# Gate tiles as a stage of their own in seven-product form, attention in one row of 32 steps with the Fourier output product between its pieces

## What is computed

```
hx    = modulate(rms_norm(x, norm1_g), sh1, sc1)
fx, qx, kx, vx = split_projection(hx @ w_in)            # 4 x 512 columns
qx, kx = axial_rope(rms_norm(qx)), axial_rope(rms_norm(kx))
y_four = real(fft2(fx))                                 # 4 groups of 128 channels, over 1024 tokens
y_attn = neighbourhood_attention(qx, kx, vx, kc, vc, rpb)   # 8 heads of 64, window 8 rows x 16 columns, and 256 context keys
gates  = sigmoid(hx @ w_gate)                           # 1024 x 1024 by 1024 x 2048, halves g_f and g_a
merged = g_f * (y_four @ w_fo) + g_a * (y_attn @ w_ao)
x      = x + g1 * (merged @ w_o)
x      = x + g2 * sqrelu_mlp(modulate(rms_norm(x, norm2_g), sh2, sc2))
```

## Time and profile before

| | |
|---|---|
| median of 3 runs | 2571.37 us (2571.21 to 2572.49) |
| span of the profiled execution | 2569.7 us, which is 1.7 us under the median (no time of its own is given for it) |
| PE busy | 2551.7 us, 99% of the span |
| DVE busy | 1753.3 us, 68% |
| ACT busy | 1186.7 us, 46% |
| POOL busy | 208.6 us, 8% |
| DMA | 406.66 MB, mean 158 GB/s |

### The profile page before, as it was taken

The page is one execution under the profiler, slowest core; times in us unless marked ns, Lnnn a source line. Parts: engine busy times, 40 slices in busy tenths (PEclk is TensorE's granted clock), DMA queues, the critical chain, the costliest instruction groups (busy, mean ns, idle before and its releaser), DMA issues.

```text
span 2569.7 us, 41859 instructions
## 1 busy us (share of the span) xinstructions
PE 2551.7 (99%) x16868; PEld 2146.6 (84%) x16868; DVE 1753.3 (68%) x2491; ACT 1186.7 (46%) x1870; POOL 208.6 (8%) x248
## 2 busy tenths in 40 slices
PE   8999999999999999999999999999999999999999
PEld 7888888887888888888989778977887888888887
DVE  7555554569999979798625664666667777778563
ACT  6454445545444443457332443344545555554331
POOL 2232222300000001022000000000000000000000
PEclk9999999999999999999999999999999999999999
DMA  4212211236777799962433221121642444497763
GB/s 160 75 51 77 66 42 35 91 111 199 239 256 250 276 372 321 342 245 85 150 106 99 72 74 51 54 74 54 237 153 93 157 148 156 148 349 257 250 221 135
DMA packets 290913, 406.66 MB, mean 158 GB/s; under 512 B 15776, under 2 KB 162720, under 8 KB 290720
## 3 DMA queue, kind: packets, MB, share of 16 engines
q1 hardware_dynamic: 276464, 352.07, 40.2%
q0 software_dynamic: 14256, 51.91, 6.0%
HBM read 314.79 MB, written 89.13 MB: 157 GB/s over the span
## 4 chain that ended last, share of the span: by engine, by line
PE 79%; DVE 2%; ACT 1%; issue 0%; DMA 0%; DVEq 0%; ACTq 0%; SPq 0%
PE ps L1006 22%; PE ps L939 7%; PE ps L937 7%; PE ps L941 7%; PE ps L609 3%; PE ps L593 3%; PE ps L596 3%; PE ps L1193 3%; PE ps L719 2%; PE ps L723 2%; PE ps L721 2%; PE ps L1194 2%; PE ps L1198 2%; PE ps L1168 1%; PE ps L1021 1%; PE ps L1147 1%
## 5 line engine op out<-in xcount | busy, mean ns | idle before, releaser
L937 PE MATMUL ps<-Bh,Ah 128*128 128x512 f32 x896 | 349.6, 390 | 1.4 <-ACT vb L1764 1.4
L939 PE MATMUL ps<-Bh,Al 128*128 128x512 f32 x896 | 348.8, 389 | 1.5 <-DVE Al L2400 1.5
L2163 DVE TENSOR_TENSOR Wlo<-Wraw,Whi 128x1024 fp32r<-128x1024 f32 x100 | 122.4, 1240 | 206.8 <-ACT Whi L1566 206.3
L941 PE MATMUL ps<-Bl,Ah 128*128 128x512 f32 x640 | 249.0, 389 | 0.0
L1786 ACT ACTIVATE ftr_h<-ftr_r 128x1024 fp32r<-128x1024 f32 x112 | 118.8, 1060 | 241.5 <-DMA ftr_r<-b_scratch 241.5
L719 PE MATMUL ps<-Whi,Hh 128*128 128x256 f32 x736 | 212.2, 288 | 0.0
L1006 PE MATMUL ps<-ftr_h,wgt_h 128*128 128x512 f32 x848 | 210.1, 390 | 0.0
L1006 PE MATMUL ps<-ftr_l,wgt_h 128*128 128x512 f32 x848 | 209.4, 389 | 0.0
L1006 PE MATMUL ps<-ftr_h,wgt_l 128*128 128x512 f32 x848 | 209.4, 389 | 0.0
L723 PE MATMUL ps<-Whi,Hl 128*128 128x256 f32 x736 | 208.2, 283 | 0.0
L721 PE MATMUL ps<-Wlo,Hh 128*128 128x256 f32 x736 | 208.2, 283 | 0.0
(11 more groups left out here) (390 smaller groups left out, 5471.7 us busy)
## 6 DMA issues: line engine op xcount, KB each, us to landing
b_scratch<-qb SPq DMA_DIRECT2D x224, 256.0 KB, 3.0
wgt_r<-in_m_w SPq DMA_DIRECT2D x112, 512.0 KB, 4.5
ftr_r<-b_scratch SPq DMA_DIRECT2D x112, 512.0 KB, 6.0
pair<-in_m_w SPq DMA_DIRECT2D x128, 256.0 KB, 3.3
Wraw<-in_w_in SPq DMA_DIRECT2D x56, 512.0 KB, 4.1
mraw<-in_w_ada POOLq DMA_DIRECT2D x48, 512.0 KB, 4.4
mraw<-in_m_w1T POOLq DMA_DIRECT2D x32, 512.0 KB, 6.4
other<-in_m_w SPq DMA_DIRECT2D x32, 512.0 KB, 5.3
```

What stands on the lines that cost most here:

```text
L937: e.matmul(o, h[:, k, :], Bh[x][:, k, :], start=first and k == 0, stop=False, skip_group_check=not first)
L939: e.matmul(o, l[:, k, :], Bh[x][:, k, :], start=False, stop=False, skip_group_check=not first)
L941: i = e.matmul(o, h[:, k, :], Bl[x][:, k, :], start=False, stop=k == 3, skip_group_check=not first)
L2163: e.tensor_tensor(Wlo[n % 4][:], Wraw[n % 2][:], Whi[n % 4][:].bitcast(F), ALU.subtract).then_inc(*S("w_lo", "v").tick(n))
```

## The change

- The gates leave the attention steps. They become a stage of 56 products of 12 matmuls (`SEQG`, eight columns of seven) between the channel part and the projections, with 672 matmuls of 512 columns in place of 768. The sums of activation blocks that it needs (`Th`/`Tl` 5, 6, 7, 4) are made by POOL, DVE and ACT before and during it: 10 DVE operations of 128x2048, 4 ACT copies of 128x2048, on POOL 4 of 128x512 and 2 of 128x2048. Weight blocks come in quarters of 256 KB, with the same sums on DVE as in the MLPs, and three of four outputs are added on DVE from copies that ACT makes.
- The result of the channel part is no longer split at once: ACT copies it to `Yr`, one transfer of 2048 KB writes it to `y_scratch`, since its place is needed, and one of 2048 KB reads it back (`Yb`) when the projections are done. Then ACT makes `Yh` and DVE `Yl`.
- The projections of both halves come first, then all 32 attention steps in one row. `pv` comes a step later (two buffers `pt`). Between the two `tr` of a step stands a piece of 6 matmuls of the Fourier output product (`fo_piece`), a half tile in two steps.
- ACT copies 768 columns of the first head's transposed probabilities instead of 256, DVE only those of the second head.
- Weights of `w_ao` are fed at steps 8, 16 and 24 by all three engines.

```diff
+        SEQG = [(x, 0) for x in (1, 5, 6, 2, 7)]
+        for q in range(1, 8):
+            SEQG += [(1, q), (5, q), (4, q - 1), (6, q), (3, q - 1), (2, q), (7, q)]
+        SEQG += [(4, 7), (3, 7)]
+        NG = len(SEQG)
+        GSTEP = {x: s for s, x in enumerate(SEQG)}
+        GOUT = {2: (0, 0, 0), 7: (1, 1, 1), 4: (2, 1, 0), 3: (3, 0, 1)}
...
+            def gate_product(s):
+
+                x, q = SEQG[s]
+                if x == 1:
...
+                elif x in (6, 7, 4):
+                    pe.wait_ge(S("gate_copy").at(GSTEP[{6: 1, 7: 6, 4: 7}[x], q]))
+                elif x == 3:
+                    pe.wait_ge(S("gc_sum").at(4 * q + 1))
...
+                pe.wait_ge(S("a_part_hi").at((1, s)), S("a_part_lo").at((1, s)))
+                if x > 3:
+                    pe.wait_ge(S("t_hi").at((5, 6, 7, 4).index(x)), S("t_lo").at((5, 6, 7, 4).index(x)))
+                for k, (bh, bl) in enumerate(of):
+                    e.matmul(o, h[:, k, :], bh, start=first and k == 0, stop=False, skip_group_check=not first)
+                    e.matmul(o, l[:, k, :], bh, start=False, stop=False, skip_group_check=not first)
+                    i = e.matmul(o, h[:, k, :], bl, start=False, stop=k == 3, skip_group_check=not first)
+                i.then_inc(*S("ps_full", b).tick(key))
...
+            def fo_piece(p):
+
+                i, late = divmod(p, 2)
+                m, hf = divmod(i, 2)
+                if i % 4 == 0 and not late:
+                    fo_w[0] = weight(("w_fo", m), 4)
+                n, wh, wl = fo_w[0]
+                t, c, ms = psum[3][:, 512:1024], HALF[hf], slice(128 * (m % 2), 128 * (m % 2) + 128)
+                if not late:
+                    if i:
+                        pe.wait_ge(S("fo_free").at(i - 1))
+                    else:
+                        empty(3, filled[3])
+                    pe.wait_ge(S("w_hi").at(n), lo_of(n))
+                for k in ((2, 3) if late else (0, 1)):
+                    pe.wait_ge(S("fy_hi").at(k), S("fy_lo").at(k))
+                    e.matmul(t, wh[:, k, ms], Yh[:, k, c], start=k == 0, stop=False)
+                    e.matmul(t, wl[:, k, ms], Yh[:, k, c], start=False, stop=False)
+                    x = e.matmul(t, wh[:, k, ms], Yl[:, k, c], start=False, stop=k == 3)
+                if late:
+                    x.then_inc(*S("fo_full").tick(i))
+                    GL[n] = i
...
-                pe.wait_ge(S("kcT").at(0), S("vc").at(0))
-                for i in range(NP):
-                    qk(half, i)
-                    for g in gate_steps(half, i) or [None]:
-                        steps_ = iter(()) if g is None else gate(half, g)
-                        next(steps_, None)
-                        if i:
-                            tr(half, i - 1, 0)
-                        next(steps_, None)
-                        if i:
-                            tr(half, i - 1, 1)
-                        next(steps_, None)
-                        if i:
-                            pv(half, i - 1)
+            for i in range(NP):
+                qk(i)
+                if i:
+                    tr(i - 1, 0)
+                    fo_piece(i - 1)
+                    tr(i - 1, 1)
+                if i > 1:
+                    pv(i - 2)
+            fo_piece(NP - 1)
...
+            sp.wait_ge(*(out_at(("chan", par, j)) for par, j in CHAN))
+            e.dma_start(y_d, Yr[:]).then_inc(*S("y_out").tick(0, 16))
+            for s in range(NG):
+                gate_step(*SEQG[s])
+                if s >= 3:
+                    gate_out(s - 3)
...
+            sp.wait_ge(full_at(((1, "v"), 1)), S("y_out").at(0))
+            e.dma_start(Yb[:], y_d).then_inc(*S("y_in").tick(0, 16))
+            for i in range(1, NP + 1):
+                pair = (i - 1) // 8 + 1
+                if i % 8 == 4 and pair < 4:
+                    sp.wait_ge(S("soft_max").at((i - 1, 1)))
+                    load_bias(pair, be, "be", biasE)
+                if i % 8 == 0 and pair < 4:
+                    sp.wait_ge(S("soft_max").at((i - 1, 1)))
+                    load_bias(pair, bm, "bm", biasM)
+                if i % 2 == 0:
+                    fo_out(i // 2 - 1)
+                    if i % 8 == 0:
+                        feed(upto(("w_fo", i // 4 - 2)))
...
+            def gate_copy(s):
+
+                x, q = SEQG[s]
+                if x not in (1, 6, 7, 4):
+                    return
+                act.wait_ge(gproduct_full(s), S("y_out").at(0))
+                if x == 4:
+                    if q >= 2:
+                        act.wait_ge(S("moved", 2 + 4 * (q % 2)).at((2, q - 1)))
+                    e.activation(gst[q % 2][2][:], psum[q % 2][:, HALF[0]], ACT.Copy).then_inc(*S("gate_copy").tick(s))
+                    return
+                back = 2 if x == 6 else 1
+                if q >= back:
+                    act.wait_ge(S("gc_sum").at(4 * (q - back) + {1: 0, 6: 3, 7: 1}[x]))
+                e.activation({1: p1b, 6: gwb[q % 2], 7: gvb}[x][:], psum[q % 2][:, HALF[0]], ACT.Copy).then_inc(
+                    *S("gate_copy").tick(s))
+
+            ga_part(0)
+            chan_out(1, 0)
+            ga_part(1)
+            ga_part(2)
+            chan_out(0, 1)
+            t_hi(7)
+            chan_out(1, 1)
+            for n in range(NG + 1):
+                if n:
+                    gate_copy(n - 1)
+                if n + 3 < NG:
+                    ga_part(n + 3)
+                if n == 4:
+                    t_hi(4)
...
+            table(LOG)
+            for i in range(NP):
+                if i > 2:
+                    o_out(i - 3)
+                if i:
+                    turned(i - 1, 0)
+                soft(i, 0)
+                if i:
+                    turned(i - 1, 1)
+                soft(i, 1)
+                if i == 0:
+                    for k in range(4):
+                        fy_hi(k)
+                elif i % 2 == 0:
+                    fo_copy(i // 2 - 1)
+                if i and i % 8 == 0:
+                    feed(upto(("w_fo", i // 4 - 2)))
...
+            t_lo(5)
+            dve.wait_ge(full_at(("ctx_k1", "T")), H2.lo_at(7))
+            t_part(0, Tr[6][:], block(Hh, 4, 1), Tr[5][:], ALU.subtract)
+            e.tensor_tensor(Tr[6][:], Tr[6][:], block(Hl, 4, 1), ALU.add).then_inc(*S("t_raw").tick((1, 1)))
...
+            ga_sum(1)
+            ga_part(0)
+            dve.wait_ge(S("t_pool").at((1, 0)))
+            t_part(1, Tr[7][:], block(Hh, 4, 1), block(Hh, 0, 1), ALU.subtract)
+            e.tensor_tensor(Tr[7][:], Tr[7][:], Tlow[:], ALU.add).then_inc(*S("t_raw").tick((2, 1)))
+            ga_part(1)
+            ga_sum(2)
+            ga_part(2)
+            t_lo(7)
...
+            for i in range(NP):
+                if i:
+                    norm(i - 1, 1)
+                soft(i, 0)
+                soft(i, 1)
+                if i:
+                    turned(i - 1)
+                norm(i, 0)
+                if i == 0:
+                    for k in range(4):
+                        fy_lo(k)
+                elif i % 8 == 0:
+                    feed(upto(("w_fo", i // 4 - 2)))
...
+            for k in range(4):
+                pool.wait_ge(S("normed").at((5, 0, k)), S("normed").at((5, 1, k)))
+                i = e.tensor_tensor(Tr[5][:, k, :], HT[:, k, HALF[1]], HT[:, k, HALF[0]], ALU.subtract)
+                i.then_inc(*S("t_pool").tick((0, k)))
+            pool.wait_ge(S("xs").at(7), S("t_hi").at(0), S("t_lo").at(0), S("t_raw").at((1, 0)))
             for b in range(2):
                 e.memset(g4(Z[0][1][b])[:, :, 0].bitcast(F), 0.0).then_inc(*S("z_zero").tick(b))
+            block = lambda t, rows, tokens: t[:, rows:rows + 4, HALF[tokens]].bitcast(F)
+            pool.wait_ge(full_at(("dft", 1, 1)), H2.lo_at(7))
+            e.tensor_tensor(Tlow[:], block(Hl, 4, 1), block(Hl, 0, 1), ALU.subtract).then_inc(*S("t_pool").tick((1, 0)))
+            pool.wait_ge(full_at(("chan", 0, 1)))
+            e.tensor_tensor(Tr[4][:], block(Hh, 4, 0), block(Hl, 4, 0), ALU.add).then_inc(*S("t_pool").tick((2, 0)))
...```

How the order changes at three places. First ACT, from the last DFT outputs to the start of what follows the channel part. Before (`Yh` is the channel result, `fo` the output tiles):

```order
L1991 ACTIVATE Z_247<-ps 128x1024
L1977 ACTIVATE Yh<-ps 128x4x256 [waits s_ps_full_0]
L1999 ACTIVATE Z_241<-mid_259 128x4 [waits s_mid_hi]
L1977 ACTIVATE Yh<-ps 128x4x256 [waits s_ps_full_1]
L1977 ACTIVATE Yh<-ps 128x4 [waits s_ps_full_2]
L1977 ACTIVATE Yh<-ps 128x4x255
L1977 ACTIVATE Yh<-ps 128x4x256 [waits s_ps_full_3]
L1566 ACTIVATE Whi_55<-Wraw_53 128x1024 [waits s_ps_full_1,s_w_raw_0]
L2010 ACTIVATE fo_261<-ps 128x1024 [waits s_ps_full_0]
L2010 ACTIVATE fo_262<-ps 128x1024
L1566 ACTIVATE Whi_56<-Wraw_54 128x1024 [waits s_ps_full_3,s_w_raw_1]
```

(36 more changed lines are left out.)

602 lines of the change are left out of this document (331 added, 271 removed).

## The result

The changed kernel takes 2599.8 us (median; 2598.7 to 2602.2) against 2571.9 us: 1.011 times as long, 95% interval 1.0096 to 1.0125. The profiled execution spans 2598.7 us where that of before spans 2569.7, 29.0 us more. The forecast was 2593.9 (2560 to 2617), slower with 0.81.

The account below looks back on a forecast made before the run. The prediction took PE, busy 99% of the span, as the bound. Its terms, -32.0 + 5.3 + 9.4 + 14.3 + 19.2 + 0 + 6.3 = +22.5 us, moved the median from 2571.4 to 2593.9 us, range 2560 to 2617.

Parts of the forecast that it names:

- PE's own work: Whole kernel: 96 matmuls fewer (21.8 us) and less loss where kinds of matmul alternate, together 32.0 us off PE.
- term of 10.2 us for alternation: Attention steps: loss where kinds of matmul alternate falls from 0.47 to 0.15 us, 32 x 0.32 = 10.2 us less.
- Ahead of the channel part: Before Hl and the DFT: POOL sums slow DVE, and added sums delay the DFT's third weight; +5.3 us, bounds 0 and 8.
- The third gate product: Gate stage: PE waits for the p1b copy, which stands behind the write to y_out; +9.4 us, bounds 4.5 and 14.
- The start of the row: First attention steps: the read of Yb, its splits, norm and soft leave PE idle 14.3 us, bounds 10.6 and 19.6.
- the read half hidden, the splits not: Start of the attention row: the lower bound of that wait, 10.6 us.
- Three weights in the row: Steps 8, 16, 24: issue, landing and splits of a weight idle PE 3 x 6.4 = 19.2 us, bounds 0 and 24.
- The rest of the row: Other attention steps: PE bounds them against DVE and ACT, at zero waits.
- hand-overs bound the row: Rival, attention steps: DVE and PE so close that half a microsecond a step is lost; +14 us, 2608, chance 0.13.
- Half rate: Matmuls after the two longest waits (gate product, row start) run at half rate: 2 x 3.15 = 6.3 us, bounds 0 and 15.8.
- the slow rate comes back after every wait: Rival: half rate also follows the three weight waits in the row, adding 3 x 3.15 us; 2603, chance 0.13.
- The landings are hidden: Rival: 29.6 us of transfer landings (write, read of Yb, three weights) are hidden; sum -13.4 us, 2558, chance 0.13.

Follow-up runs that it names:

- sixth experiment: Changed kernel with the sums for Tr5 and Tr4 made by VectorE instead of GpSimd: 2596.1 us, 1.0093 times the kernel before.
- fifth experiment: Changed kernel without the four Yl operations of VectorE, PE multiplying Yh twice instead: 2596.1 us, 1.0091 times the kernel before.
- first experiment: Changed kernel with the three attention-row weights split five steps later (13, 21, 29), loads issued where they were: 2583.6 us, 1.0046 times the kernel before.

## Why the prediction was right, and where its sizes were off

The direction and the places were right; the sum was 6.5 us short on the span (22.5 against 29.0). By its parts:

1. *PE's own work*, -32.0: measured about -25.7. The 96 matmuls fewer hold, and so do gate products 2.72 us apart (the fourth starts at 1327.82, the fifth at 1330.55). The step that failed is the term of 10.2 us for alternation, "I take 0.15 for the one remaining alternation". Without any gain there an edge step would be 10.02 - 24 x 0.227 + 1.36 = 5.93 us and a middle step 6.61; they take 5.80 and 6.50. So 0.12 us a step came back in these two (0.10 over eight steps on end) and not 0.32: 3.3 to 3.9 us in all. The experiment with the doubled piece shows that the other 0.2 is PE's and no hand-over: with six or with twelve matmuls in the piece, an edge step takes 0.33 us above the 4.11 of `qk`, `tr` and `pv` and 0.227 a matmul. Each of these still follows one of another kind. A price per change of kind would fit (seven changes for 0.47 us before, five for 0.33 now), but no run varies their number alone, so this is not shown.

2. *Ahead of the channel part*, +5.3: the channel matmuls start 7.2 us later than in the earlier trace rows, of which 0.7 is there before this stage: 6.5. The eight `HT` rows were slowed by 4.1 us, as forecast (4.3), but they and not the `Hl` rows met GpSimd, and PE has no slack before the weights that ScalarE splits behind the last `Hh`, where I had counted 1.6 us of slack before the last `Hl`. The sixth experiment shows the cause.

3. *The third gate product*, +9.4 and 3.15 at half rate: the stage takes 14.3 us above 152.3, of which 9.1 and 2.3 are this wait and the slow matmuls behind it, and 1.5 the one before the second product. The write was faster than taken (6.3 us to landing, not 7.8), but began 20.8 us behind the start of the channel part and not 18.3, since GpSimd's `Tr4` held up an `Al` of VectorE for 5.1 us. That hold-up also makes the wait before the second product (1.5 us by its row), which I did not have. So 9.1 against 9.4 is luck in part, errors that cancel; without the hold-up, in the sixth experiment, this wait is 6.5 us.

4. *The start of the row*, +14.3 and 3.15: 13.8 with the half rate in it (qk to qk, less the matmuls in between), 9.4 of it waits. The chain in the forecast went through the landing of `Yb`. It is hidden: the fifth experiment takes VectorE's splits away and gains 4.6 us with the same read. The bound from below, "the read half hidden, the splits not", was the better guess. It left out the first softmax altogether: the 5.5 us before `qk` of step 1 are that, behind two weight splits.

5. *Three weights in the row*, +19.2: 19.1, and 0.6 in step 18. The first experiment gives all of it back there, and takes 0.8 for each weight in a later step. PE is idle 13.3 us in them and not 19.2; the other 5.8 are `tr` and `pv` at half rate. The forecast let the whole delay reach PE, but `norm` has room: in the first experiment's trace it is ready at 1683.88 and the second `tr` starts at 1686.46, 2.6 us later. So the sum agrees only because two errors cancel.

6. *The rest of the row*, zero: right. The rival "hand-overs bound the row" is refuted by the doubled piece.

7. *Half rate*, +6.3: about 14 us of matmul time in all (0.9 before the DFT, 2.3, 4.4, 5.8, and 0.6 in step 18), by steps that are longer than waits and full-rate matmuls explain. Twelve slow matmuls cost 2.3 us more, not the 3.15 taken from the earlier trace rows. The rival "the slow rate comes back after every wait" described the mechanism better than the forecast did. By the Trainium skill (page "TensorE: Matmul & The Clock Gate", Part 1) an array that stood idle comes back at half clock; the trace agrees, with granted clocks of 0.53 and 0.62 behind the waits. Only its price was smaller than the matmuls' own lengthening: filling the waits gave back 3.7 us and not 8.

Waits alone were forecast at 48.2 us and measured at about 40; the half rate at 6.3 and about 14. These two nearly cancel, which is luck. The miss is the alternation term, with 0.7 us lost before all this and some 0.4 us that I can't place. "The landings are hidden" fails for two of three landings: the write and the weights were in PE's way, the read of `Yb` was not.
